# Wider spacing of the operand rows that TensorE reads, in a 256-token two-block network on one core

## What is computed

```python
def first_block(x, ...):            # 2 layers
    proj = x @ w_in                 # 2048 -> 10304, state-space mixer
    ...
    h = yg @ w_out                  # 4096 -> 2048
    x = layer_norm(ALPHA * x + h)
    proj = x @ w_in                 # 2048 -> 4944, sparse attention
    q = c_q @ w_uq                  # 512 -> 4096; then w_uk, w_uv per head
    h = (o * silu(gate)) @ w_out    # 4096 -> 2048
    x = layer_norm(ALPHA * x + h)

def second_block(x, ...):           # 2 layers
    proj = rms_norm(h) @ w_in       # 2048 -> 12288, gated MLP
    h = h + y @ w_out               # 4096 -> 2048
    proj = rms_norm(h) @ w_in       # 2048 -> 8192, stick-breaking attention
    h = h + o @ w_out               # 2048 -> 2048
    return rms_norm(h)
```

## Time and profile before

| | |
|---|---|
| time, median of 3 runs | 2435.77 us (2435.55 to 2437.74) |
| profiled execution, first to last instruction (span) | 2435.7 us |
| TensorE matmul, weight load, share of the span | 100%, 96% |
| VectorE, ScalarE, GpSimd | 65%, 51%, 4% |
| DMA queue of the loads | 60.9% of 16 engines |
| granted TensorE clock, mean | 0.999 |
| moved | 467.93 MB, 192 GB/s |

### The profile page before, as it was taken

How to read it: one execution, slowest core, us unless ns; L and a number is a source line. 1 busy time by engine, 2 the same in 40 slices (tenths; PEclk the granted TensorE clock), 3 DMA queues, 4 the chain that set the end, 5 groups by cost and what they waited for, 6 DMA issues and landing times.

```text
span 2435.7 us, 45481 instructions
## 1 busy us (share of the span) xinstructions
PE 2423.8 (100%) x19626; PEld 2341.2 (96%) x19626; DVE 1571.2 (65%) x2109; ACT 1243.2 (51%) x1426; POOL 90.5 (4%) x68
## 2 busy tenths in 40 slices
PE   9999999999999999999999999999999999999998
PEld 9999999999999999999988899999999999999998
DVE  6778878866577776666575555655655555555556
ACT  5445665554454565554464444544544445455453
POOL 0001000110021000000000000000000000000002
PEclk9999999999999999999999999999999999999999
DMA  7665656657755645546757666666555576555645
GB/s 238 198 196 180 210 180 187 185 174 236 232 175 174 199 150 165 152 150 231 232 185 244 190 203 198 187 186 197 180 190 186 190 233 208 184 171 178 188 161 182
DMA packets 267434, 467.93 MB, mean 192 GB/s; under 512 B 18955, under 2 KB 70497, under 8 KB 265313
## 3 DMA queue, kind: packets, MB, share of 16 engines
q1 hardware_dynamic: 267233, 465.02, 60.9%
HBM read 452.18 MB, written 4.26 MB: 187 GB/s over the span
## 4 chain that ended last, share of the span: by engine, by line
PE 98%; DVE 1%; ACT 0%; issue 0%; DMA 0%; SPq 0%; ACTq 0%
PE G L703 91%; PE M L703 5%; PE M L716 1%; DMA RAW<-in_ssd_w_in 0%; DVE W2m L1546 0%; DVE W0m L1546 0%; DVE E L1639 0%; ACT W0m L1125 0%; DVE E L1680 0%; DVE SZ L1708 0%; DVE E L1641 0%; ACT L1205 0%; DVE W L1546 0%; DVE W1m L1546 0%; ACT YY L1131 0%
## 5 line engine op out<-in xcount | busy, mean ns | idle before, releaser
L703 PE MATMUL G<-AA,W 128*128 128x256 f32 x7908 | 942.6, 277 | 1.1 <-DVE W L1546 1.0
L703 PEld LDWEIGHTS G<-AA,W 128*128 128x128 f32 x7908 | 917.9, 188 | 7.3 <-issue 4.1
L1546 DVE TENSOR_TENSOR W<-RAW,W 128x1024 fp32r<-128x1024 f32 x446 | 557.4, 1251 | 370.6 <-ACT W L1125 369.4
L1125 ACT CAST W<-RAW 128x1024 fp32r<-128x1024 f32 x446 | 464.8, 1047 | 467.7 <-PE G L703 457.8
L703 PE MATMUL G<-AA,WY 128*128 128x256 f32 x2508 | 305.3, 278 | 0.0
L703 PEld LDWEIGHTS G<-AA,WY 128*128 128x128 f32 x2508 | 293.2, 188 | 2.5 <-issue 2.2
L1546 DVE TENSOR_TENSOR WY<-RAW,WY 128x1024 fp32r<-128x1024 f32 (+1 forms) x112 | 140.8, 1259 | 74.9 <-ACT WY L1125 74.9
L703 PE MATMUL G<-W0m,YY 128*128 128x256 f32 x1512 | 183.8, 276 | 1.0 <-DVE W0m L1546 1.0
L703 PE MATMUL G<-W1m,YY 128*128 128x256 f32 x1512 | 182.9, 276 | 0.1
L703 PE MATMUL G<-W,YY 128*128 128x512 f32 x792 | 181.3, 389 | 0.0
L703 PE MATMUL G<-W2m,YY 128*128 128x256 f32 x1488 | 180.5, 276 | 0.0
(11 more groups left out here) (306 smaller groups left out, 2398.0 us busy)
## 6 DMA issues: line engine op xcount, KB each, us to landing
RAW<-in_a_w_in SPq DMA_DIRECT2D x192, 512.0 KB, 3.8
RAW<-in_ssd_w_in SPq DMA_DIRECT2D x160, 512.0 KB, 4.4
RAW<-in_b_w_in SPq DMA_DIRECT2D x128, 512.0 KB, 4.1
RAW<-in_dsa_w_in SPq DMA_DIRECT2D x72, 512.0 KB, 3.6
RAW<-in_ssd_w_out SPq DMA_DIRECT2D x64, 512.0 KB, 4.6
RAW<-in_dsa_w_out SPq DMA_DIRECT2D x64, 512.0 KB, 4.1
RAW<-in_a_w_out SPq DMA_DIRECT2D x64, 512.0 KB, 3.6
RAW<-in_b_w_out SPq DMA_DIRECT2D x32, 512.0 KB, 3.7
```

The source lines that it names most:

```text
L703: return e.matmul(o, l, r, start=start, stop=stop, skip_group_check=True)
L1125: e.copy(wh[:, 0:n], RAW[:, v % NR, 0:n]).then_inc(*up(cast_done, "cast", v))
L1546: e.tensor_tensor(wl[:, 0:n], RAW[:, v % NR, 0:n], wh[:, 0:n].bitcast(F), ALU.subtract).then_inc(*up(rest_done, "rest", v))
```

## The change

Between two rows of `AA` there are now 3 unused numbers (12 bytes): row r of its 32 begins at 496 + 12 r modulo 512. For ordinary units in slots 0 to 2 a third view `W3S` of the slot holds 16 tiles (8 of heads, 8 of rests) with 5 unused numbers (20 bytes) behind each: tile s begins at 128 + 20 s. The unit's matmuls, its cast and its subtraction go through that view, the last two as 8 pieces of 128 columns. Units of cq, v5, v7, v and o1 to o4, and all lent slots, keep their form. The 16 x 20 = 320 bytes fit into the 368 that lie behind each slot for the second view; the 32 x 12 = 384 of `AA` move the small constant buffers behind it by 384 bytes, and `YY` and all that follows stay where they were. No instruction is added, removed or moved: the order of each engine's instructions is the same.

```diff
--- before.py
+++ after.py
@@ -243,12 +243,14 @@
         return nc.alloc_sbuf_tensor_at(name, shape, dt, offset=off, align_bytes=4)
 
     RAW = place("RAW", [P, NR, UW])
-    W3, W3M = [], []
+    W3, W3M, W3S = [], [], []
     for i in range(3):
         W3.append(place(f"W{i}", [P, 2 * UW], R, line=STILL))
-        W3M.append(place(f"W{i}m", [P, 2 * UW], R, top[0] - 8 * UW + MOVING - STILL))
+        w_at = top[0] - 8 * UW
+        W3M.append(place(f"W{i}m", [P, 2 * UW], R, w_at + MOVING - STILL))
+        W3S.append(place(f"W{i}s", [P, 16, P + 5], R, w_at))
         top[0] += MOVING - STILL
-    AA = place("AA", [P, 16, 2, T], R, line=MOVING)
+    AA = place("AA", [P, 16, 2, T + 3], R, line=MOVING)[:, :, :, 0:T]
     TB = place("TB", [P, 2])
     ident = place("ident", [P, P])
     ones = place("ones", [P, P])
@@ -350,6 +352,15 @@
             return W7[:, 0:UW], W7[:, UW:2 * UW]
         k = 24 if s == "z1" else 28
         return WY[k][:, 0:UW], WY[k][:, UW:2 * UW]
+
+    def spaced(u):
+        return plan.slot[u] in (0, 1, 2) and units[u][0][0] not in TOKENS + ("v",)
+
+    def tiles_of(u):
+        if spaced(u):
+            w = W3S[plan.slot[u]][:, :, 0:P]
+            return w[:, 0:8, :], w[:, 8:16, :]
+        return [w.rearrange("p (s n) -> p s n", n=P) for w in pair_of(u)]
 
     def used(u):
         n, w = len(units[u][3]), units[u][2]
@@ -730,14 +741,13 @@
             if name == "k":
                 if i == 0:
                     e.wait_ge(*on("ck"))
-                wh = wh.rearrange("p (h c n) -> p h c n", h=4, c=2)
-                wl = wl.rearrange("p (h c n) -> p h c n", h=4, c=2)
+                wh, wl = tiles_of(u)
                 for h in range(4):
                     o = G[:, half + h // 2, (h % 2) * T:(h % 2 + 1) * T]
                     for c in range(2):
-                        mm(o, wh[:, h, c, :], CK[:, c, 0, :], c == 0 and h % 2 == 0, False)
-                        mm(o, wh[:, h, c, :], CK[:, c, 1, :], False, False)
-                        last = mm(o, wl[:, h, c, :], CK[:, c, 0, :], False, c == 1)
+                        mm(o, wh[:, 2 * h + c, :], CK[:, c, 0, :], c == 0 and h % 2 == 0, False)
+                        mm(o, wh[:, 2 * h + c, :], CK[:, c, 1, :], False, False)
+                        last = mm(o, wl[:, 2 * h + c, :], CK[:, c, 0, :], False, c == 1)
                 last.then_inc(*up(unit_done, "unit", u))
                 return
             if name == "v":
@@ -759,6 +769,7 @@
                 e.wait_ge(*on("copied", s, kts[0] // 2))
                 X = AS
             n = len(kts)
+            th, tl = tiles_of(u)
             wh = wh[:, 0:n * width].rearrange("p (k n) -> p k n", k=n)
             wl = wl[:, 0:n * width].rearrange("p (k n) -> p k n", k=n)
             nk = units[us[-1]][1][-1] + 1
@@ -785,7 +796,7 @@
                 else:
                     for f in range(width // P):
                         o = G[:, half + f // 2, (f % 2) * T:(f % 2 + 1) * T]
-                        h, l = wh[:, j, f * P:(f + 1) * P], wl[:, j, f * P:(f + 1) * P]
+                        h, l = (w[:, j * (width // P) + f, :] for w in (th, tl))
                         mm(o, h, X[:, k, 0, :], k == 0 and f % 2 == 0, False)
                         mm(o, h, X[:, k, 1, :], False, False)
                         last = mm(o, l, X[:, k, 0, :], False, k == nk - 1)
@@ -1122,7 +1133,12 @@
                 elif plan.slot[v] == "x7":
                     e.wait_ge(*on("end6", "dve"))
                     e.wait_ge(*on("end6", "pe"))
-                e.copy(wh[:, 0:n], RAW[:, v % NR, 0:n]).then_inc(*up(cast_done, "cast", v))
+                if spaced(v):
+                    th, _ = tiles_of(v)
+                    e.copy(th[:, 0:n // P, :], RAW[:, v % NR, 0:n].rearrange("p (s n) -> p s n", n=P)).then_inc(
+                        *up(cast_done, "cast", v))
+                else:
+                    e.copy(wh[:, 0:n], RAW[:, v % NR, 0:n]).then_inc(*up(cast_done, "cast", v))
 
         def head(dst, src, *event):
             return e.copy(dst, src).then_inc(*up(act_made, *event))
@@ -1543,8 +1559,14 @@
                 n = used(v)
                 wh, wl = pair_of(v)
                 e.wait_ge(*on("cast", v))
-                e.tensor_tensor(wl[:, 0:n], RAW[:, v % NR, 0:n], wh[:, 0:n].bitcast(F), ALU.subtract).then_inc(
-                    *up(rest_done, "rest", v))
+                if spaced(v):
+                    th, tl = tiles_of(v)
+                    e.tensor_tensor(tl[:, 0:n // P, :], RAW[:, v % NR, 0:n].rearrange("p (s n) -> p s n", n=P),
+                                    th[:, 0:n // P, :].bitcast(F), ALU.subtract).then_inc(
+                                        *up(rest_done, "rest", v))
+                else:
+                    e.tensor_tensor(wl[:, 0:n], RAW[:, v % NR, 0:n], wh[:, 0:n].bitcast(F),
+                                    ALU.subtract).then_inc(*up(rest_done, "rest", v))
 
         def rest(dst, src, head):
             return e.tensor_tensor(dst, src, head.bitcast(F), ALU.subtract)
```

## The result

The changed kernel takes 2491.34 us (median of 4 runs, 2491.06 to 2492.55) against 2436.36 us of the kernel before on the same chip (2435.55 to 2437.74). The ratio is 1.0229, with a 95% interval of 1.0216 to 1.0241: slower by 55 us, where 42 were forecast.

A forecast was written before the change was run, and what follows sets the result against it. The prediction took TensorE's matmul pace to bound the kernel; +42 us from stationary tiles, all other terms 0, on 2435.7 us gave 2478 us. The range was 2402 to 2498 us, the likeliest case's own 2455 to 2500.

The forecast's parts named there:

- What bounds the kernel: Whole kernel: TensorE is busy throughout at 2.4 GHz, so only the pace of its matmuls counts, not when data is ready.
- Stationary tiles off 128: Products with spaced weight tiles in slots 0 to 2: 7,843 matmuls lose 5.4 ns each, +42.4 us.
- four combinations: Large products before the change: moving at 496 or 128, stationary at 128: floor; moving at 128 or 496, stationary at 496: slower.
- Moving rows off 496, tile left at 128: The 3,036 matmuls with WY and Wx: taken as 0, or +10 us if the pace never settles.
- `AA` stationary with weights moving: cq, first parts of v5 and v7: 240 matmuls with W, 132 with lent slots; 0, ends 2.5 us either way.
- Cast and subtraction in pieces: Slot preparation in 8 pieces of 128 columns: taken as 0, since waiting units cover any longer work on VectorE.
- the copies: Copies of AA into YY, reading pieces of 1,024 bytes instead of 4,096: taken as 0, with +12 us as the end.
- No change: Rival for all large products: TensorE's two reads are independent of their addresses, time stays at 2436 us; chance 0.15.
- A shorter settling: Rival at 206 places after side work: spread addresses end bad meetings at once, 8 us less, 2428 us; chance 0.17.
- a lower floor: Rival for 11,592 matmuls: spread addresses avoid part of a repeated collision, 3.3 ns less each, -38 us, 2397 us; chance 0.13.

## Why the prediction was right, and where its reason was not

- **What bounds the kernel**: right. Only TensorE's pace moved, the granted clock stayed at 0.999, and no wait took its place.
- **Stationary tiles off 128** (7,843 x 5.4 = +42.4 us): the size was right, for a wrong reason. In the changed kernel the matmuls of slots 0 to 2 take 39.3 + 2.8 = 42.1 us more. That the sum came out so close is in part luck: the spaced tiles alone cost +39, 4.6 ns on each of 8,556 matmuls, but the rows alone cost 39.5 us on the 7,908 of the same matmuls with `AA`, where the prediction would have put nothing. I concluded from four combinations that "the stationary address decides and the moving one hardly matters". Moving rows at 0, 176 or 508 against tiles at 128 cost 46 to 53 us, and a stationary operand at 4 costs nothing with the weights moving at 128. The four combinations were too few, and two of them came from another width.
- **Moving rows off 496, tile left at 128** (taken as 0, with +10 as the end): this is the step that failed. The matmuls with `WY` and `Wx` take 13.4 us more, 4.4 ns each, where the forecast put nothing and allowed 10 at the most. The forecast of 42.4 was 12 us short of the 54.4 of the profiled execution, and this term makes that up. The upper end was set by a mean over 24 matmuls that includes settled ones, while a steady pair off the cheap one loses 5 to 11 ns in each matmul (118.3 ns at (176, 128), 124.0 at (4, 128)).
- **`AA` stationary with weights moving** (0, at most 2.5 us): in the stretch below, of the changed kernel, 36 of them take 8.46 us, 235.0 ns each, where 60 took 233.3 before. At 1.7 ns the 372 would come to under a microsecond; over the whole trace they take 0.1 us less.

```profile
1279.96 8.63 PE L714 MATMUL G<-W,AA 128*128 128x512 f32 x36
1288.42 1.78 PE L714 MATMUL G<-WB,AA 128*128 128x512 f32 x7
```

- **Cast and subtraction in pieces, and the copies** (0): right, as the rows of the result show.
- **No change**: ruled out by every run that only moves a buffer. The same instructions on the same data take from 2436 to 2531 us by the addresses alone, so TensorE's pace with these two reads is not independent of their addresses. The Trainium skill (TensorE: Matmul & The Clock Gate, Step-by-step: what each phase is for) gives each of them a port of its own; whatever the ports, the paces of 113.3, 118.3 and 124.0 ns differ by the addresses only.
- **A shorter settling, a lower floor**: neither was seen. The 24 matmuls that took 2.80 and 2.78 us after side work take 2.86 and 2.87 in the changed kernel, and no 24 large products in a row with 256 columns are under 113.3 ns in any trace. Spread addresses visit mostly expensive pairs in turn and never stay on one, where the kernel before sits on a cheap one.

What sets a pair's pace is shown only as far as this: it depends on both addresses, it is steady over whole stretches, it is reached only after some matmuls, and it can have two values for one pair, as for (320, 128) and (508, 128). That the two reads collide in the memory would fit this, but no run shows a collision or where it would be; the mechanism is open.

## What to carry to other kernels

In a kernel bound by fp32r matmuls like this one, the start addresses of the moving row and of the stationary tile are a tuning parameter: here they were worth 0.6 to 3.9% of the whole kernel, and neither alignment nor an even spread was a guide to it. Put all rows and all tiles on one measured pair by padding every buffer to a fixed address modulo 512. If both must move, move them together and measure again; here shifts of 32 and 64 bytes kept the pace and one of 20 lost it. Spacing that is meant to spread accesses takes a tuned kernel off its pair; time one constant shift before spacing rows.

## What the runs showed that I had not expected

- Twelve bytes of shift of `AA` alone cost 53 us (2488.6 against 2435.8), twenty bytes of both buffers 95 us (2530.6 against 2435.4).
- The costs of two misplaced operands don't add: +55 and +39 alone, +55 together.
- Moving rows that change address at two of three matmuls, ones that change it every 12, and ones constant at 508 take the same time within 4 us (2490.5, 2492.4, 2488.6).
- The pair (320, 128) holds either of two paces, 113.3 and 117.8 ns, for whole units, and (508, 128) either of 117.8 and 120.0.
- Twelve matmuls at the cheap pair (496, 128) are too few to reach its pace: they still run at 118.6 ns.
